# Down products by tokens in the second FFN, with the residual transposed into the banks and the last stage by tokens

## The chip, the cores and the metric

The kernel runs on one core of one Trainium2 chip. Its metric is the device time of one execution, in microseconds (us), given as the median of several runs. Engines are TensorE (PE; PEld is its weight load), VectorE (DVE), ScalarE (ACT), GpSimd (POOL) and SyncE (SP), which issues most DMAs.

## The reference, cut to what matters

Two transformer blocks on 256 tokens of width 1024. The change touches the end of the second: a gated FFN with a causal convolution (2816 hidden channels) and the per-layer gate behind it.

```python
    u = causal_dwconv(rmsnorm_2(x, g_ffn) @ w_up, ffn_conv_w)
    u_gate, u_val = jnp.split(u, 2, axis=-1)
    x = x + (jax.nn.silu(u_gate) * u_val) @ w_down

    x = x + jax.nn.sigmoid(rmsnorm_2(x, g_ple) @ w_ple_gate) * (p_i.astype(x.dtype) @ w_ple)
    return x
```

`rmsnorm_2(x, g)` is x times g over the root of the mean square of a token's 1024 channels. All is float32.

## The kernel before

**Arithmetic.** Each float32 operand of a large product is split in two parts, `hi` (fp32r) and `lo` (the rest). `product` (lines 1076 to 1081) makes three matmuls of one product: its first operand is stationary in TensorE, its second moves, hi by hi (L1079), hi by lo (L1080) and lo by hi (L1081).

**Layout.** The residual `XT` is held by channels: partition = channel within a tile of 128, free dimension = tile and 256 tokens. In `gemm` a weight tile of 128x128 is stationary and 256 tokens move. A chunk of weights is 2048 columns for each partition (1 MB). Chunks pass through three rings of three buffers: SP loads `raw`, ACT writes `whi` (`split_hi`, L572), DVE writes `wlo` (`split_lo`, L581). `adv(name)` splits the chunk that lies three places behind `name`; it waits until `name`'s products are done, by `multiplied`.

**Second FFN.** For each of 11 steps `j`: gate chunk `sg`, value chunk `sa` (48 matmuls each, in a ring of two banks, 0 and 1), then the down chunk `sd` of step j-2 (`down`: 2 tiles `t` of hidden channels by 8 output tiles `nb` by 3 matmuls, accumulated over all steps in banks 4 to 7, each bank holding two output tiles by 256 tokens). ACT and DVE run the convolution and the silu. Ahead of it stand the sum of squares `sum4` (`sum_squares`, L1113) and ten filler products `keep_clock` (L1118), during which the residual is normalised.

**Last stage, as PE issues it.** The products of `p` by `w_ple` (`ple`, four units a to d of 12 matmuls), with the sum of squares `sum5` between b and c; four filler products; the gate products `pg0` to `pg3` (48 matmuls each); 16 transposes of the sum (L1694). Beside it DVE adds the down banks to `XT` (`add_x`, L2426); ACT squares them (L772); ACT takes the root (L607) and DVE the reciprocal of 128x256 values (L1726); DVE scales (L1736), ACT writes the hi parts (`norm_hi`, L622), DVE the lo parts (L1746), and only then can the gate products start. At the end ACT takes the sigmoid of each gate unit (L909, 128x512), DVE multiplies (L2477) and adds (L2478), PE transposes to tokens, ACT (L1043) and DVE (L2481) copy out of the banks, and SP stores two halves of 512 KB (L518).

Each engine runs its instructions in program order; all waits are on semaphores.

Of the kernel before, what the change touches and what calls it, by code (L numbers as in the profile page):

```python
# [22 lines left out]
ALU = mybir.AluOpType  # L23
# [6 lines left out]
P = 128  # L30
# [71 lines left out]
def build(nc, i, out):  # L102
# [66 lines left out]
    for c in range(4):  # L169
        chunk(f"pg{c}", cols(i["w_ple_gate_2"][0], 256 * c), (KT, 256))  # L170
    N_SPLIT = sum(not c[0] for c in CHUNKS)
# [34 lines left out]
    g_units += [(f"s{n}{j}", "dve") for j in range(FFT // 2) for n in "ga"]  # L206
    g_units += [(f"ple{c}", "act") for c in "abcd"] + [(f"pg{c}", "act") for c in range(4)]
    l_units = [(f"sa{n}", "dve") for n in range(2)] + [(f"sb{n}", "dve") for n in range(4)]
# [11 lines left out]
    m_units += [(n, "act") for n in ("lq0", "lq1", "lk0", "lk1", "sfq0", "sfq1", "sfk0", "sfk1")]  # L220
    m_units += [("pT", "dve"), ("on2", "act"), ("on3", "act"), ("sum4", "act"), ("sum5", "act")]

    with ExitStack() as ctx:
# [124 lines left out]
        PF = slot(16, 1, 0, 512)  # L348
        PLE = slot(18, 2).rearrange("p (k t) -> p k t", t=T)
        SMY, SMA, RB, NCF = (slot(19, 1, 256 * n, 256) for n in range(4))  # L350
# [13 lines left out]
        OUTN = slot(4, 2).rearrange("p (a d) -> p a d", a=2)  # L364
        PG = slot(2, 2).rearrange("p (k t) -> p k t", t=T)
        SQ2 = slot(0, 2)
        nf2 = small[:, 72:80]
        gain2 = small[:, 64:72]
# [42 lines left out]
        def multiplied(g):  # L411

            name = [n for n, k in G.items() if k == g][0]
            if name[0:2] in ("fd", "sd") and name[2:].isdigit():
                return down_used, int(name[2:]) + 1 + (FFT // 2 if name[0] == "s" else 0)
            unit = [n for n, _ in g_units if n == name or n[:-1] == name and n[-1] in "abcd"][-1]
            return g_full, g_no(unit) + 1
# [17 lines left out]
        def m_done(u):  # L435
# [16 lines left out]
            sem(n) for n in ("x_init", "y_f32", "y_hi", "y_lo", "p_hi", "p_lo", "merged_f32", "osq2", "qd_exp"))  # L452
        out_act, out_dve, acc2_start, silu2 = (sem(n) for n in ("out_act", "out_dve", "acc2_start", "silu2"))
        u2_f32 = sem("u2_f32")
# [7 lines left out]
        def _(sp):  # L462
# [71 lines left out]
        def _(pool):  # L534
# [51 lines left out]
        def _(act):  # L586
# [439 lines left out]
            def ple(n):  # L1026
                u = f"ple{'abcd'[n]}"
                g_wait(u)
                act.activation(PLE[:, 2 * n:2 * n + 2, :], two(g_bank(u)), ACT.Copy).then_inc(g_empty["act"], 1)
            squares(lambda c: (x_new, 8 + c + 1), dst=SQ2)  # L1030
            ple(0)
            ple(1)
            norm_std("sum5", T, D)
            ple(2)
            ple(3)
            norm_hi(HT2, 18)
            adv("sd10")
            adv("ple")
            for c in range(4):
                copy_unit(f"pg{c}", PG[:, 2 * c:2 * c + 2, :], ACT.Sigmoid)  # L1040
            for n in range(2):
                act.wait_ge(l_full, len(l_units) + 2 * n + 1)
                act.activation(OUTN[:, n, 0:512], bank[4 + 2 * n][:, :], ACT.Copy).then_inc(out_act, 1)  # L1043


        @block.tensor
        def _(pe):
# [608 lines left out]
            sum_squares("sum4", 8, T, SQ2)  # L1656
            keep_clock(bank[4], 10)
            for j in range(FFT // 2):
                if j == 0:
                    gemm_first("sg0", T, 20)  # L1660
                else:
                    gemm(f"sg{j}", T)
                gemm(f"sa{j}", T)
                if j > 1:
                    down(j - 2, "s")
            down(FFT // 2 - 2, "s")
            down(FFT // 2 - 1, "s")

            def ple(units):

                wh, wl = w_parts("ple", 2)
                for u in units:
                    o = g_open("ple" + u)
                    for n in range(2):
                        nb = 2 * "abcd".index(u) + n
                        for k in range(2):
                            ws = [x[:, k, P * nb:P * (nb + 1)] for x in (wh, wl)]
                            ins = product(o[:, T * n:T * (n + 1)], ws, (phi[:, k, :], plo[:, k, :]), k == 0, k == 1)
                    ins.then_inc(g_full, 1)
            pe.wait_ge(p_hi, 1)  # L1680
            pe.wait_ge(p_lo, 1)
            ple("ab")
            sum_squares("sum5", 12, T, SQ2)
            ple("cd")
            keep_clock(bank[4], 4)
            gemm_first("pg0", T, 24)
            for c in range(1, 4):
                gemm(f"pg{c}", T)

            for t in range(2):  # L1690
                for c in range(2):
                    pe.wait_ge(x_new, 12 + 2 * (c + 1))
                    for k in range(4):
                        ins = pe.transpose(bank[4 + 2 * t + c][:, P * k:P * (k + 1)],  # L1694
                                           XT[:, 4 * c + k, P * t:P * (t + 1)], ident)
                    ins.then_inc(l_full, 1)


        @block.vector
        def _(dve):  # L1700
# [764 lines left out]
            adv(f"sd{FFT // 2 - 2}")  # L2465
            for c in range(4):
                dve.wait_ge(*((down_bank, 4 + c) if c < 3 else (down_used, FFT)))
                add_x(2 * c, bank[4 + c]).then_inc(x_new, 1)
            dve.wait_ge(x_new, 12)
            normalise(HT2, 24, T, XT[:, :, 0:T], lambda k, n: par("g_ple", k=k), None, "sum5")  # L2470
            adv("sd10")
            adv("ple")
            for c in range(4):
                s_ = slice(2 * c, 2 * c + 2)
                adv(f"pg{c}")
                dve.wait_ge(*g_done(f"pg{c}"))
                link(dve.tensor_tensor(PG[:, s_, :], PG[:, s_, :], PLE[:, s_, :], ALU.mult))  # L2477
                dve.tensor_tensor(XT[:, s_, 0:T], XT[:, s_, 0:T], PG[:, s_, :], ALU.add).then_inc(x_new, 1)  # L2478
            for n in range(2):
                dve.wait_ge(l_full, len(l_units) + 2 * n + 2)  # L2480
                dve.tensor_copy(OUTN[:, n, 512:1024], bank[5 + 2 * n][:, :]).then_inc(out_dve, 1)  # L2481

# [24 lines left out]
```

## Time and profile before

| | us |
|---|---|
| median of 3 runs | 1045.29 (1043.66 to 1047.16) |
| profiled execution, its own time | 1041.31 |
| its span, first to last instruction | 1039.5 |
| PE busy in the span | 982.0 (94%) |
| DVE busy | 763.5 (73%) |
| ACT busy | 504.5 (49%) |

The profiled execution is 3.98 us below the median of the runs, and 1.81 us of its own time lie outside its span. The mean granted TensorE clock is 0.99 of full speed. A matmul's row gives its latency; matmuls overlap, so what one costs is the distance between starts.

### The profile page before, as it was taken

How to read it: one execution, taken by the hardware profiler on the slowest of the kernel's cores; microseconds unless marked ns; L12 is line 12 of the kernel's file. 1: busy time of each engine (PE TensorE's matmuls, PEld its weight loads, DVE VectorE, ACT ScalarE, POOL GpSimd, SP SyncE). 2: the span in 40 equal slices, each digit the busy share in tenths (PEclk: the TensorE clock that was granted, in tenths of full speed). 3: DMA queues.
4: the chain of work that ended last, by engine and by line, in shares of the span. 5: the costliest groups of instructions: out<-in, count | busy, mean ns of one | idle time of the engine just before them, and what ended most of it. 6: DMA issues, size and time to landing. Idle time of an engine off the chain costs nothing.

```text
span 1039.5 us, 17879 instructions
## 1 busy us (share of the span) xinstructions
PE 982.0 (94%) x7608; PEld 937.9 (90%) x7608; DVE 763.5 (73%) x1106; ACT 504.5 (49%) x619; POOL 14.8 (1%) x31
## 2 busy tenths in 40 slices
PE   5899999998899999998998999999989999999997
PEld 3478999898899999998897889999989999999997
DVE  5679997877978898867959967544675776666664
ACT  5544434525554565447734553323544645454552
POOL 0000000002000000000100000000000000000000
PEclk9999999999999999999999999999999999999999
DMA  9787443345275567656766774635454455555521
GB/s 339 239 287 246 154 162 116 129 155 173 95 253 188 190 209 243 163 122 122 134 166 107 172 161 90 117 90 107 130 183 142 143 183 191 174 192 173 195 89 41
DMA packets 144094, 170.57 MB, mean 164 GB/s; under 512 B 3120, under 2 KB 133440, under 8 KB 144016
## 3 DMA queue, kind: packets, MB, share of 16 engines
q1 hardware_dynamic: 142112, 165.63, 54.5%
q10 hardware_dynamic: 1200, 2.43, 0.6%
q0 software_dynamic: 704, 1.39, 0.5%
q8 instruction: 60, 0.98, 0.4%
q14 instruction: 18, 0.15, 0.0%
HBM read 168.37 MB, written 1.05 MB: 163 GB/s over the span
## 4 chain that ended last, share of the span: by engine, by line
PE 58%; DVE 11%; ACT 4%; issue 3%; DMA 2%; DVEq 0%; ACTq 0%
PE bank L1079 17%; PE bank L1080 17%; PE bank L1081 17%; PE bank L1549 4%; DVE wlo L581 3%; ACT whi L572 2%; DMA raw<-in_w_in_dram 2%; DVE arena L2191 1%; DVE arena L2059 1%; DVE arena L1736 1%; DVE arena L2152 1%; PE bank L1113 1%; DVE arena L2221 1%; DVE arena L1726 1%; ACT arena L916 0%
## 5 line engine op out<-in xcount | busy, mean ns | idle before, releaser
L1079 PE MATMUL bank<-hhi,whi 128*128 128x256 f32 (+1 forms) x2000 | 581.7, 291 | 23.9 <-DVE arena L2152 4.8
L1080 PE MATMUL bank<-hlo,whi 128*128 128x256 f32 (+1 forms) x2000 | 574.8, 287 | 0.0
L1081 PE MATMUL bank<-hhi,wlo 128*128 128x256 f32 (+1 forms) x2000 | 574.6, 287 | 0.0
L1079 PEld LDWEIGHTS bank<-hhi,whi 128*128 128x128 f32 x2000 | 385.5, 193 | 33.7 <-issue 24.0
L581 DVE TENSOR_TENSOR wlo<-raw,whi 128x2048 fp32r<-128x2048 f32 x131 | 299.6, 2289 | 144.2 <-ACT whi L572 103.8
L1080 PEld LDWEIGHTS bank<-hlo,whi 128*128 128x128 f32 x2000 | 385.6, 193 | 3.8 <-issue 1.2
L1081 PEld LDWEIGHTS bank<-hhi,wlo 128*128 128x128 f32 x2000 | 385.5, 193 | 2.5
L572 ACT ACTIVATE whi<-raw 128x2048 fp32r<-128x2048 f32 x131 | 250.3, 1911 | 123.5 <-PE bank L1081 69.1
L2059 DVE SCALAR_TENSOR_TENSOR arena<-arena,params 128x256 f32<-128x256 f32 x176 | 71.5, 479 | 5.8 <-ACT arena L801 5.8
L2444 DVE SCALAR_TENSOR_TENSOR arena<-bank,params,arena 128x255 f32<-128x255 f32 (+1 forms) x88 | 36.4, 476 | 31.9 <-ACT arena L1012 31.6
L909 ACT ACTIVATE arena<-bank 128x512 f32<-128x512 f32 x22 | 13.2, 598 | 91.9 <-PE bank L1081 91.9
L1012 ACT ACTIVATE arena<-bank,params 128x256 f32<-128x256 f32 x44 | 18.5, 470 | 61.1 <-PE bank L1081 61.1
L1549 PE MATMUL bank<-arena 128*128 128x128 f32 x336 | 40.0, 275 | 1.4 <-DVE arena L2321 1.4
L1549 PEld LDWEIGHTS bank<-arena 128*128 128x128 f32 x336 | 38.8, 192 | 1.6 <-DVE arena L2321 1.6
L1079 PE MATMUL bank<-whi,hhi 128*128 128x256 f32 x128 | 37.1, 290 | 0.0
L1081 PE MATMUL bank<-whi,hlo 128*128 128x256 f32 x128 | 36.2, 283 | 0.0
L1080 PE MATMUL bank<-wlo,hhi 128*128 128x256 f32 x128 | 36.2, 283 | 0.0
L772 ACT ACTIVATE arena<-XT 128x512 f32<-128x512 f32 x16 | 10.0, 631 | 42.7 <-DVE XT L2023 23.2
L1827 DVE SCALAR_TENSOR_TENSOR raw<-raw,small 128x256 f32<-128x256 f32 x72 | 29.5, 480 | 0.0
L1079 PEld LDWEIGHTS bank<-whi,hhi 128*128 128x128 f32 x128 | 24.5, 192 | 0.2 <-issue 0.2
L1080 PEld LDWEIGHTS bank<-wlo,hhi 128*128 128x128 f32 x128 | 24.5, 192 | 0.2 <-issue 0.2
L1081 PEld LDWEIGHTS bank<-whi,hlo 128*128 128x128 f32 x128 | 24.5, 192 | 0.0
(326 smaller groups left out, 886.7 us busy)
## 6 DMA issues: line engine op xcount, KB each, us to landing
raw<-in_w_in_dram SPq DMA_DIRECT2D x46, 1024.0 KB, 8.4
raw<-in_w_up_dram SPq DMA_DIRECT2D x44, 1024.0 KB, 5.1
raw<-in_w_down_dram SPq DMA_DIRECT2D x22, 1024.0 KB, 4.9
raw<-in_w_ada_dram SPq DMA_DIRECT2D x19, 1024.0 KB, 5.3
raw<-in_w_branch_dram SPq DMA_DIRECT2D x6, 1024.0 KB, 5.1
arena<-in_w_ada_dram SPq DMA_DIRECT2D x10, 512.0 KB, 9.3
raw<-in_w_out_dram SPq DMA_DIRECT2D x4, 1024.0 KB, 5.1
raw<-in_w_o_dram SPq DMA_DIRECT2D x4, 1024.0 KB, 5.1
```

The lines of the kernel that those rows point to most:

```text
L572: act.activation(whi[:, g % RING, :], raw[:, n % RING, :], ACT.Copy).then_inc(w_hi, 1)
L581: dve.tensor_tensor(wlo[:, g % RING, :], raw[:, n % RING, :], whi[:, g % RING, :].bitcast(F32), ALU.subtract).then_inc(w_lo, 1)
L909: act.activation(dst, two(g_bank(u)), func).then_inc(g_empty["act"], 1)
L1012: ins = act.activation(acc2[:, b, n, t, :], g_bank(f"s{w}{j}")[:, T * t:T * (t + 1)], ACT.Copy, scale=col)
L1079: pe.matmul(o, wh, ah, start=start, stop=False, **kw)
L1080: pe.matmul(o, wh, al, start=False, stop=False, **kw)
L1081: return pe.matmul(o, wl, ah, start=False, stop=stop, **kw)
L1113: ins = pe.matmul(o[:, 0:w], ones, src[:, w * k:w * (k + 1)], start=k == 0, stop=k == KT - 1)
L1549: ins = pe.matmul(o[:, P * h:P * (h + 1)], lhsT(c, h), rhs(c, h), start=True, stop=True)
L1827: ins = dve.scalar_tensor_tensor(out=w[:, k % 2, :], in0=w[:, k, :], scalar=silu_c[:, k, 0:1], in1=w[:, k % 2, :], op0=ALU.mult, op1=ALU.add)
L2059: ins = dve.scalar_tensor_tensor(out=a, in0=pad[:, b, t, dy:dy + 4, dx:dx + 64], scalar=par("conv_w", k=FFT * tap + 2 * j + t), in1=a, op0 ...
L2444: ins = dve.scalar_tensor_tensor(out=acc2[:, b, n, t, d:T], in0=ps[:, T * t:T * (t + 1) - d], scalar=par("ffn_conv", k=2 * FFT * (2 - d) + ...
```

## The change

- `down_tokens` takes the place of `down` in the second FFN: a slice of 128 tokens of `u` is stationary, and 512 columns of the down weights move. A chunk is 2 tiles `t` by 2 token halves `a` by 2 column halves `c` by 3 = 24 matmuls. Banks 4 to 7 now hold 128 tokens by 512 channels.
- The residual is not added by DVE at the end: ahead of the FFN, behind `sum4`, 16 transposes put it into banks 4 to 7 (the first of each bank starts it), and the down products accumulate on top. Filler products there go from ten to six.
- The last stage is by tokens. DVE makes `XG` = bank times `g_ple` (a row spread over all partitions by a new DMA that POOL issues behind `sum4`). ACT sums squares of the banks with `accum_out`, takes a root of 2 columns, DVE a reciprocal of 2 columns. PE transposes `XG` (`tokens_turn`, four units of 4 transposes); ACT and DVE split the result. The reciprocal root is not multiplied in ahead of the gate products; it is the `scale` of the sigmoid. `sum5`, the four filler products, `normalise` and `norm_hi` of this stage go.
- `ple` and the gate products have tokens stationary and 512 columns moving (24 and 96 matmuls for all). The gate chunks are cut as 4 row tiles by 512 columns. Gate units are `gate{c}{t}`: column half c, token half t; both banks of a c are opened ahead of its first product.
- The sum with the bank is written by DVE straight to `OUTN`, with no transposes and no copies, and stored in four pieces of 256 KB.

```diff
-    m_units += [("pT", "dve"), ("on2", "act"), ("on3", "act"), ("sum4", "act"), ("sum5", "act")]
+    m_units += [("pT", "dve"), ("on2", "act"), ("on3", "act"), ("sum4", "act")] + [(f"hT{n}", "dve") for n in range(4)]
...
-            for t in range(2):
-                sp.wait_ge(out_act, t + 1)
-                sp.wait_ge(out_dve, t + 1)
-                sp.dma_start(o[:, t, :], OUTN[:, t, :]).then_inc(stored, 16)
-            sp.wait_ge(stored, 32)
+            for c in range(2):
+                for t in range(2):
+                    sp.wait_ge(out_dve, 2 * c + t + 1)
+                    s = slice(512 * c, 512 * (c + 1))
+                    sp.dma_start(o[:, t, s], OUTN[:, t, s]).then_inc(stored, 16)
+            sp.wait_ge(stored, 64)
...
+            pool.wait_ge(m_full, m_no("sum4") + 1)
+            r = ROWS["g_ple"]
+            pool.dma_start(ple_gain, i["table"][r:r + 8, :].rearrange("r f -> (r f)").partition_broadcast(P)
+                           ).then_inc(gain_loaded, 16)
...
+            square_sums(0)
+            adv("sd10")
             ple(0)
             ple(1)
-            norm_std("sum5", T, D)
+            tokens_hi(0)
             ple(2)
             ple(3)
-            norm_hi(HT2, 18)
-            adv("sd10")
+            tokens_hi(1)
             adv("ple")
-            for c in range(4):
-                copy_unit(f"pg{c}", PG[:, 2 * c:2 * c + 2, :], ACT.Sigmoid)
-            for n in range(2):
-                act.wait_ge(l_full, len(l_units) + 2 * n + 1)
-                act.activation(OUTN[:, n, 0:512], bank[4 + 2 * n][:, :], ACT.Copy).then_inc(out_act, 1)
+            square_sums(1)
+            act.wait_ge(std5_ready, 1)
+            act.activation(rstd5, rstd5, ACT.Sqrt, bias=eps, scale=1.0 / D).then_inc(std5_ready, 1)
+            adv("pg0")
+            act.wait_ge(rstd5_ready, 1)
+            for c in range(2):
+                for t in range(2):
+                    u = f"gate{c}{t}"
+                    g_wait(u)
+                    act.activation(PG[:, t, 512 * c:512 * (c + 1)], g_bank(u)[:, :], ACT.Sigmoid,
+                                   scale=rstd5[:, t:t + 1]).then_inc(g_empty["act"], 1)
...
-            keep_clock(bank[4], 10)
+            pe.wait_ge(*g_done("wp3"))
+            for t in range(2):
+                for c in range(2):
+                    for k in range(4):
+                        pe.matmul(bank[4 + 2 * t + c][:, P * k:P * (k + 1)], XT[:, 4 * c + k, P * t:P * (t + 1)],
+                                  ident, start=k == 0, stop=False, is_transpose=True, skip_group_check=True)
+            keep_clock(m_bank("hT0"), 6)
+
+            def down_tokens(j):
+
+                b = j % 3
+                wh, wl = w_parts(f"sd{j}", 2)
+                pe.wait_ge(u_hi, FFT // 2 + j + 1)
+                pe.wait_ge(u_lo, FFT // 2 + j + 1)
+                last = j == FFT // 2 - 1
+                order = [(t, a, c) for a in range(2) for c in range(2) for t in range(2)] if last else \
+                        [(t, a, c) for t in range(2) for a in range(2) for c in range(2)]
+                for t, a, c in order:
+                    tok = [u[:, b, t, P * a:P * (a + 1)] for u in (uhi, ulo)]
+                    ws = [x[:, t, 512 * c:512 * (c + 1)] for x in (wh, wl)]
+                    ins = product(bank[4 + 2 * a + c][:, :], tok, ws, False, last and t == 1, skip_group_check=True)
...
             ple("ab")
-            sum_squares("sum5", 12, T, SQ2)
+            tokens_turn(0)
             ple("cd")
-            keep_clock(bank[4], 4)
-            gemm_first("pg0", T, 24)
-            for c in range(1, 4):
-                gemm(f"pg{c}", T)
-
-            for t in range(2):
-                for c in range(2):
-                    pe.wait_ge(x_new, 12 + 2 * (c + 1))
-                    for k in range(4):
-                        ins = pe.transpose(bank[4 + 2 * t + c][:, P * k:P * (k + 1)],
-                                           XT[:, 4 * c + k, P * t:P * (t + 1)], ident)
-                    ins.then_inc(l_full, 1)
+            tokens_turn(1)
+
+            for c in range(2):
+                o = [g_open(f"gate{c}{t}")[:, :] for t in range(2)]
+                for part in range(2):
+                    wh, wl = w_parts(f"pg{2 * c + part}", 4)
+                    for t, k in [(t, k) for t in range(2) for k in range(4)]:
+                        kk = 4 * part + k
+                        if c == 0 and k == 0:
+                            pe.wait_ge(h_hi, 24 + 2 * t + part + 1)
+                            pe.wait_ge(h_lo, 24 + 2 * t + part + 1)
+                        ins = product(o[t], acts(T, kk, P * t, P), [x[:, k, :] for x in (wh, wl)], kk == 0,
+                                      kk == KT - 1, skip_group_check=True)
...
+            dve.wait_ge(gain_loaded, 16)
+            for n in range(4):
+                dve.wait_ge(*((down_bank, 4 + n) if n < 3 else (down_used, FFT)))
+                s_ = slice(512 * (n % 2), 512 * (n % 2) + 512)
+                dve.tensor_tensor(XG[:, n // 2, s_], bank[4 + n][:, :], ple_gain[:, s_], ALU.mult).then_inc(x_new, 1)
             adv("sd10")
...
+            tokens_lo(0)
+            tokens_lo(1)
             adv("ple")
...
+            dve.wait_ge(ss5_ready, 4)
+            dve.tensor_tensor(rstd5.unsqueeze(2), ss5.rearrange("p (a c) -> p a c", c=2)[:, :, 0:1],
+                              ss5.rearrange("p (a c) -> p a c", c=2)[:, :, 1:2], ALU.add).then_inc(std5_ready, 1)
+            dve.wait_ge(std5_ready, 2)
+            dve.reciprocal(rstd5, rstd5).then_inc(rstd5_ready, 1)
+            adv("pg0")
+            for c in range(2):
+                for t in range(2):
+                    s_ = slice(512 * c, 512 * (c + 1))
+                    dve.wait_ge(*g_done(f"gate{c}{t}"))
+                    link(dve.tensor_tensor(PG[:, t, s_], PG[:, t, s_], PLE[:, t, s_], ALU.mult))
+                    dve.tensor_tensor(OUTN[:, t, s_], PG[:, t, s_], bank[4 + 2 * t + c][:, :], ALU.add
+                                      ).then_inc(out_dve, 1)
```

## Rows read from the trace of the kernel before

**Rows 1.** The page, busy time and share of the span for each engine.

```profile
PE 982.0 (94%) x7608; PEld 937.9 (90%) x7608; DVE 763.5 (73%) x1106; ACT 504.5 (49%) x619; POOL 14.8 (1%) x31
```

**Rows 2.** Windows: stretch, length, busy PE PEld DVE ACT POOL, clock, DMA share, GB/s.

```profile
40.00:50.00 10.00, 8.08 (x34) 4.22 (x35) 4.01 (x3) 4.76 (x7) 0.00 (x0) 0.83 0.11 31
817.00:995.00 178.00, 178.00 (x1486) 178.00 (x1485) 119.63 (x138) 87.43 (x96) 0.00 (x0) 1.00 0.55 184
1000.00:1039.00 39.00, 32.32 (x251) 30.88 (x249) 21.11 (x26) 15.00 (x18) 0.00 (x0) 1.00 0.07 28
```

**Rows 3.** Groups of PE's matmuls by shape; the moving operand is named first.

```profile
L1079 PE MATMUL bank<-hhi,whi 128*128 128x256 f32 x1936 | 556.7, 288 | 22.7 <-DVE arena L2152 4.8 <-issue 4.6 <-ACT whi L572 3.7
L1079 PE MATMUL bank<-whi,hhi 128*128 128x256 f32 x128 | 37.1, 290 | 0.0
L1079 PE MATMUL bank<-hhi,whi 128*128 128x512 f32 x64 | 25.1, 391 | 1.3 <-DVE hlo L1751 0.7 <-ACT arena L674 0.6
```

**Rows 4.** Timeline of PE in the first projection, matmuls of 512 columns: start, length.

```profile
59.93 0.39 PE L1081 MATMUL bank<-hhi,wlo 128*128 128x512 f32 x1
...
63.33 0.39 PE L1081 MATMUL bank<-hhi,wlo 128*128 128x512 f32 x1
64.31 0.47 PE L1079 MATMUL bank<-hhi,whi 128*128 128x512 f32 x1 [0.59 <-ACT arena L674]
```

**Rows 5.** Timeline of PE ahead of the second FFN.

```profile
797.18 3.62 PE L1113 MATMUL bank<-arena,cf 128*128 128x256 f32 x16
800.63 4.48 PE L1118 MATMUL bank<-cf 128*128 128x256 f32 x20
805.62 0.36 PE L1079 MATMUL bank<-hhi,whi 128*128 128x256 f32 x1 [0.51 <-ACT hhi L622]
```

**Rows 6.** Timeline of PE in the last stage.

```profile
995.77 0.28 PE L1079 MATMUL bank<-hhi,whi 128*128 128x256 f32 x1
...
998.65 3.62 PE L1113 MATMUL bank<-arena,cf 128*128 128x256 f32 x16
...
1007.16 0.36 PE L1079 MATMUL bank<-hhi,whi 128*128 128x256 f32 x1 [0.29 <-DVE hlo L1746]
...
1012.87 0.28 PE L1081 MATMUL bank<-hhi,wlo 128*128 128x256 f32 x1
1014.16 0.36 PE L1079 MATMUL bank<-hhi,whi 128*128 128x256 f32 x1 [1.01 <-ACT whi L572]
...
1031.38 0.28 PE L1081 MATMUL bank<-hhi,wlo 128*128 128x256 f32 x1
...
1033.80 1.53 PE L1694 MATMUL bank<-cf,XT 128*128 128x128 f32 x12 [1.70 <-DVE XT L2478]
```

**Rows 7.** Timeline of ACT around and in the last stage.

```profile
990.27 1.92 ACT L572 ACTIVATE whi<-raw 128x2048 fp32r<-128x2048 f32 x1 [3.33 <-PE bank L1081]
...
999.46 1.28 ACT L607 ACT_TABLE_LOAD   x1
...
1031.70 0.60 ACT L909 ACTIVATE arena<-bank 128x512 f32<-128x512 f32 x1 [5.16 <-PE bank L1081]
```

**Rows 8.** Timeline of DVE around and in the last stage.

```profile
992.27 2.29 DVE L581 TENSOR_TENSOR wlo<-raw,whi 128x2048 fp32r<-128x2048 f32 x1 [2.87 <-ACT whi L572]
994.48 2.48 DVE L2426 TENSOR_TENSOR XT<-bank,XT 128x512 f32<-128x512 f32 x4
...
1033.05 0.69 DVE L2478 TENSOR_TENSOR XT<-XT,arena 128x512 f32<-128x512 f32 x1
...
1035.37 0.69 DVE L2481 COPY arena<-bank 128x512 f32<-128x512 f32 x1 [0.18 <-PE bank L1694]
```

**Rows 9.** A group of ACT's accumulator reads, in the first stage.

```profile
L639 ACT ACTIVATION_READ_ACCUMULATOR arena<-arena 128x1 f32 x4 | 0.8, 188 | 0.0
```

**Rows 10.** DMA issues by source: engine, count, size, median us to landing.

```profile
out_dram<-arena SPq DMA_DIRECT2D x2, 512.0 KB, 2.8
arena<-in_w_spatial_dram SPq DMA_DIRECT2D x1, 256.0 KB, 4.9
```

More of the change, by code:

```diff
@@ L169, in build @@
     for c in range(4):
-        chunk(f"pg{c}", cols(i["w_ple_gate_2"][0], 256 * c), (KT, 256))
+        chunk(f"pg{c}", rows(i["w_ple_gate_2"][0], 4 * (c % 2), 4)[:, :, 512 * (c // 2):512 * (c // 2 + 1)], (4, 512))
     N_SPLIT = sum(not c[0] for c in CHUNKS)
@@ L206, in build @@
     g_units += [(f"s{n}{j}", "dve") for j in range(FFT // 2) for n in "ga"]
-    g_units += [(f"ple{c}", "act") for c in "abcd"] + [(f"pg{c}", "act") for c in range(4)]
+    g_units += [(f"ple{c}", "act") for c in "abcd"] + [(f"gate{c}{t}", "act") for c in range(2) for t in range(2)]
     l_units = [(f"sa{n}", "dve") for n in range(2)] + [(f"sb{n}", "dve") for n in range(4)]
@@ L1664, in _ @@
                 if j > 1:
-                    down(j - 2, "s")
-            down(FFT // 2 - 2, "s")
-            down(FFT // 2 - 1, "s")
+                    down_tokens(j - 2)
+            down_tokens(FFT // 2 - 2)
+            down_tokens(FFT // 2 - 1)
             def ple(units):
@@ L1673, in ple, with tokens_turn @@
                     o = g_open("ple" + u)
[L1674 to L1678, printed above, removed]
-                    ins.then_inc(g_full, 1)
+                    c, t = divmod("abcd".index(u), 2)
+                    s = slice(512 * c, 512 * (c + 1))
+                    for k in range(2):
+                        ws = [x[:, k, s] for x in (wh, wl)]
+                        tok = [x[:, k, P * t:P * (t + 1)] for x in (phi, plo)]
+                        ins = product(o[:, :], tok, ws, k == 0, k == 1)
+                    ins.then_inc(g_full, 1)
+            def tokens_turn(a):
+                for half in range(2):
+                    n = 2 * a + half
+                    o = m_bank(f"hT{n}")
+                    if n >= 2:
+                        pe.wait_ge(h_lo, 24 + n - 1)
+                    pe.wait_ge(x_new, 8 + n + 1)
+                    for k in range(4):
+                        ins = pe.transpose(o[:, P * k:P * (k + 1)], XG[:, a, 512 * half + P * k:512 * half + P * (k + 1)],
+                                           ident)
+                    ins.then_inc(m_full, 1)
             pe.wait_ge(p_hi, 1)
@@ L2465, in _ @@
             adv(f"sd{FFT // 2 - 2}")
[L2466 to L2470, printed above, removed]
-            adv("sd10")
-            adv("ple")
[L2473 to L2478, printed above, removed]
@@ new lines, in _, with tokens_lo @@
+            adv("sd10")
+            def tokens_lo(a):
+                for half in range(2):
+                    n = 2 * a + half
+                    dve.wait_ge(h_hi, 24 + n + 1)
+                    s_ = slice(4 * half, 4 * half + 4)
+                    dve.tensor_tensor(h_tok[1][:, s_, a, :], four(m_bank(f"hT{n}")),
+                                      h_tok[0][:, s_, a, :].bitcast(F32), ALU.subtract).then_inc(h_lo, 1)
+            tokens_lo(0)
+            tokens_lo(1)
+            adv("ple")
@@ new lines, in _ @@
+            dve.wait_ge(ss5_ready, 4)
[4 more added lines that the diff above has]
+            adv("pg0")
+            for c in range(2):
+                for t in range(2):
[4 more added lines that the diff above has]
+                                      ).then_inc(out_dve, 1)
```

39 lines of the change are left out of this document (31 added, 8 removed).

## The prediction

> **What bounds the kernel now.** I read the page's busy times first, then windows over the second FFN and the last stage, then PE's groups by shape, then the timelines of PE, ACT and DVE at the seams. PE is busy 94% of the span [rows 1]. Over the second FFN the window of 178 us shows PE busy for all 178, at a clock of 1.00, with DVE busy for 120 and ACT for 87 [rows 2]: there only PE's own work can shorten the time, and the others have about a third of theirs free. From 1000 us to the end it is otherwise: PE is busy for 32.3 of 39 us [rows 2], and the time goes into a chain through four engines. So the two places need two kinds of sum: spacing of matmuls in the one, a chain in the other.
>
> **What a matmul costs.** Its row's length (288 ns at 256 columns, 391 at 512 [rows 3]) is latency. The spacing counts: in the window 1486 matmuls start in 178.00 us, 0.120 us each [rows 2]. At 512 columns there are 15 starts between 59.93 and 63.33 us: 3.40 / 15 = 0.227 us [rows 4]. So two of 256 cost 0.240 and one of 512 costs 0.227, 0.013 less. That the weights now move does not matter by itself: the group with weights moving and tokens stationary has 290 ns against 288 [rows 3].
>
> The difference of 0.013 is what the FFN part hangs on, and a rule bears on it. The Trainium skill (TensorE: Matmul & The Clock Gate, Back-to-back issue gap) gives an isolated gap of columns / 2.4 GHz plus 2.5 ns, by which merging two matmuls saves only 2.5 ns. The rows show 13, so I go by them; by the page the sum below would be smaller by 384 pairs x 0.0108 = 4.1 us, an estimate from that page.
>
> **1. Down products.** A down chunk goes from 48 x 0.120 = 5.76 to 24 x 0.227 = 5.44 us; 11 chunks save 3.5 us. PE has no idle time there [rows 2], so all of it shows, if nothing new makes PE wait. A freed buffer is split by ACT in 1.92 and DVE in 2.29 us [rows 7, 8], 4.3 us with the hand-overs, and the chunk is wanted two chunks later (11.2 us now, 11.5 before): about 7 us of cover. The FFN's `u` is still wanted two steps later. Bounds: 0 (512 columns cost 0.240) to 3.5.
>
> **2. Ahead of the second FFN.** Transposes: 12 take 1.53 us with the latency of the last and one restart [rows 6], so 0.11 to 0.13 each, and 16 cost 1.8 to 2.0 us. Removed: 4 of 10 filler products, 4.48 us for ten [rows 5], so 1.8 us. Both lie ahead of a wait for the normalised residual that already ends last (PE idles 0.51 us, then starts at 805.62 [rows 5]): 0, bounds 0.3 either way. The gain's DMA is issued by POOL, which has nothing behind it, some 190 us before DVE wants it; a 256 KB load took 4.9 us [rows 10], so 512 KB is hidden. Uncovered it would be some 5 to 10 us.
>
> **3. Until the gate products start.** Before, from the first `ple` matmul (995.77, call it 0) to the first gate matmul (1007.16) it is 11.39 us [rows 6]: `ple` a and b 2.88, `sum5` 3.3, c and d 3.0, fillers and wait 2.2.
>
> After, by engines, same zero. DVE is late first: the lo part of `pg0` waits for ACT's, which waits for `sd9`'s products (over at -5.3): ACT to -3.3, DVE to -0.9 (before, the same pair ran from 990.27 to 994.56 [rows 7, 8]). The four `XG` products read a bank like L2426, which took 2.48 us for four [rows 8]: -0.9 to 1.5. ACT's two squares wait for the first two, each 0.63 plus an accumulator read of 0.19 [rows 9]: done at 1.4. Then the hi part of `pg1`, 1.92: 3.3. Behind it `ple` a and b are copied, 0.60 each, the length of L909 [rows 7]: 3.9 and 4.5; then the two hi copies of half 0, to 5.6. DVE makes `pg1`'s lo part to 5.7 and the lo parts of half 0 to 6.3 and 6.9. PE: `ple` a and b, 12 x 0.227 = 2.7; eight transposes to 3.7; unit c needs a's bank copied out: starts at 4.05, a stall of 0.4; c and d to 6.8; the transposes of half 1 need banks freed by DVE at 6.3 and 6.9, so they run to 7.7. First gate product at 7.8. Its second token half needs DVE again at 10.5 and has it at 9.5. Saved: 11.4 - 7.8 = 3.6 us. Bounds: 4.4, when the stall and the waits vanish (PE's own work is 5.4 + 1.8 = 7.2 us), to 2.0, when each of four hand-overs is late by 0.4.
>
> **4. The gate products.** Before, from 1007.16 to the last one's start at 1031.38 it is 24.22 us [rows 6]: 191 spacings of 0.120 = 22.9 and one stall for `pg1`'s split (1012.87 to 1014.16, 1.2 us too long [rows 6]). That stall goes, since `pg1` is split at 5.7 and wanted at 13.2. After: 95 x 0.227 = 21.6. But a new wait comes: both banks are opened before c=1, and the second is still being filled until c=0 ends. So PE waits out latency 0.39 [rows 4], a sigmoid of 0.60 [rows 7] and two hand-overs of about 0.15, less one spacing: 0.9 us; the first projection has such a wait at the same shape, 63.33 to 64.31, 0.75 too long [rows 4]. Queued behind it is all of c=1; nothing else waits. 21.6 + 0.9 + 0.1 (first matmul slow) = 22.6: 1.6 saved, bounds 0.3 (no gain by columns) to 1.8. Covered beside it: ACT's hi parts of `pg2` and `pg3`, two squares, the root and two table loads of 1.28 [rows 7], between 7.6 and 17.1, while the first gate unit is full at 16.2. So its sigmoid is about 1 us late, but the bank that PE waits for is the second, full at 19: cover 1.4 us, beyond which each late us costs one.
>
> **5. Behind the last product.** Before: from 1031.38 to DVE's last copy (1035.37 + 0.69) 4.68 us, through sigmoid, multiply, add, 12 transposes, copy [rows 6 to 8]. After: latency 0.39, sigmoid 0.60, multiply 0.69, add from the bank 0.69, three hand-overs of 0.03: 2.5. Saved 2.2 (1.9 to 2.3). The store: before, 1039.5 - 1036.06 = 3.4 us; its DMA took 2.8 to land with 512 KB, now 256 KB [rows 10]: 0.2 saved, 0 to 0.6.
>
> **Sum.** 3.5 + 0 + 3.6 + 1.6 + 2.2 + 0.2 = 11.1 us. The span goes from 1039.5 to 1028.4. The profiled execution (1041.31) stood 3.98 us below the median of the runs; I take that distance as kept: 1045.29 - 11.1 = 1034.2 us.
>
> **The rivals.**
>
> *Columns give nothing.* In the FFN, unlike in the first projection, DMA, ACT and DVE work on the rings all the time, and moving 512 columns of a ring buffer may cost 0.240. Against it: the first projection splits chunks too, and holds 0.227 [rows 4]. It gives 3.5 + 1.3 + 0.3 less: 6.0 saved, 1039.3. The page's 2.5 ns would end near there (1038.3, an estimate from the Trainium skill's TensorE: Matmul & The Clock Gate). Chance 0.12.
>
> *ACT and DVE pace the last stage.* ACT has squares, two hi parts of chunks, eight copies, roots and sigmoids in one program order, and PE's transposes wait for DVE behind it. If each hand-over in part 3 is late by its bound and the first sigmoids by 1 us beyond their cover, 2.6 us are lost: 1036.8. For it: the chain leaves DVE and PE within 0.1 us of each other at 6.9. Against: before, ACT is busy only 15 of 39 us there [rows 2]. Chance 0.14.
>
> *The clock falls (the other side).* Where PE idled and ran small work, at 40 to 50 us, the granted clock was 0.83 [rows 2]: 1.7 us' worth lost, at the lower level of 1.2 GHz half of 3.4 us. Transposes take the place of full products at two places here. One such fall costs 1.7 us, both 3.4: 1037.6. To turn the change into a loss it has to hold: at 1.2 GHz a matmul of 512 columns takes 0.427 instead of 0.227, so 14.2 us (11.1 and the 3.1 that can be told) need 71 of the last stage's 120 below. All 120 low would cost 24 us: 1058. Against it: the clock was 1.00 from 1000 to 1039 us with 16 transposes and two waits for them [rows 2, 6]. The Trainium skill (TensorE: Matmul & The Clock Gate, PE-mode transpose) says that transposes don't raise the clock as products do; no row contradicts it, and it is why this case is not at zero. One short fall 0.03, held low 0.03.
>
> **How the numbers follow.** Forecast (1032.5 to 1036.0) 0.61, columns 0.12, ACT and DVE 0.14, clock 0.06, something that no row shows 0.07. All bounds at their worst save 3.9 us (1041.4), all at their best 12.9 (1032.4); the runs of before scatter by 1.7 either way, which takes the lower end to 1030.7, and the worst of all at once is unlikely, so the range is 1030.7 to 1040.0. A measurement of this kernel can tell about 0.3%, 3.1 us. Faster by more: all but the low clock, a part of the unknown and the tail of the two mild rivals, 0.89; within it 0.07; slower 0.04.
>
> **What would show it.** Down groups of 512 columns spaced by 0.227 with no idle from 817 to some 991 us (part 1). First gate product 7.8 us behind the first `ple` matmul, with short waits for ACT's copy and for DVE's lo part (3). One wait of some 0.9 us for a sigmoid halfway through 96 gate matmuls and none for a split (4). From the last matmul's start to DVE's last add 2.5 us (5). A clock of 1.00 at both seams. It is wrong if the spacing is 0.24, if PE idles for over 1 us before the gate products, or if a window of the last stage shows a clock well under 1.

## The result and the profile after

The changed kernel takes 1028.38 us in the median of 4 runs (1026.38 to 1029.27); before, 1044.47 us beside it (4 runs). The ratio is 0.9842, 95% interval [0.9819, 0.9866]. The forecast was 1034.2, range 1030.7 to 1040.0: the way is right, and the time lies 2.3 us below the range. The profiled execution has its own time of 1029.27 and a span of 1027.5 us, 12.0 less than before's.

So two numbers want an account: the profiled spans differ by 12.0 us, where the sum gave 11.1, and the medians by 16.1.

PE's groups by shape in the changed kernel, from 800 us on, answer to [rows 3]:

```profile
L1114 PE MATMUL bank<-hhi,whi 128*128 128x256 f32 x352 | 99.6, 283 | 0.5 <-ACT hhi L635 0.5
L1114 PE MATMUL bank<-whi,hhi 128*128 128x512 f32 x128 | 50.2, 392 | 0.8 <-ACT arena L1077 0.8
```

The 128 per line are 88 of the down products, 8 of `ple` and 32 of the gates. One line has all of PE's new idle time: 0.8 us for a sigmoid. The window over the FFN answers to [rows 2]:

```profile
812.00:990.00 178.00, 178.00 (x1259) 167.91 (x1258) 122.08 (x143) 89.80 (x99) 0.00 (x0) 1.00 0.57 188
```

PE has no idle time and a clock of 1.00, as before, with 1259 matmuls in 178 us (1486 in a window of that length before). The windows over the two seams, up to PE's last matmul, have a clock of 1.00 as well:

```profile
800.00:812.00 12.00, 11.52 (x85) 10.74 (x85) 9.24 (x14) 5.19 (x8) 0.55 (x1) 1.00 0.27 94
990.00:1023.00 33.00, 32.07 (x148) 26.01 (x146) 17.69 (x20) 17.07 (x26) 0.00 (x0) 1.00 0.17 55
```

The timeline of PE at both seams answers to [rows 5, 6] (start, length):

```profile
797.23 3.62 PE L1148 MATMUL bank<-arena,cf 128*128 128x256 f32 x16
800.68 1.91 PE L1696 MATMUL bank<-cf,XT 128*128 128x128 f32 x16
802.43 2.76 PE L1153 MATMUL bank<-cf 128*128 128x256 f32 x12
805.67 0.36 PE L1114 MATMUL bank<-hhi,whi 128*128 128x256 f32 x1 [0.48 <-ACT hhi L635]
...
992.50 0.39 PE L1114 MATMUL bank<-whi,hhi 128*128 128x512 f32 x1
...
995.22 1.03 PE L1749 MATMUL bank<-cf,arena 128*128 128x128 f32 x8
996.01 0.48 PE L1114 MATMUL bank<-whi,hhi 128*128 128x512 f32 x1
...
999.75 0.47 PE L1114 MATMUL bank<-whi,hhi 128*128 128x512 f32 x1
...
1011.73 0.47 PE L1114 MATMUL bank<-whi,hhi 128*128 128x512 f32 x1 [0.82 <-ACT arena L1077]
...
1022.51 0.39 PE L1116 MATMUL bank<-whi,hlo 128*128 128x512 f32 x1
```

Ahead of the FFN nothing moved: 16 transposes (1.8 us) stand where four filler products stood, and the same wait ends at 8.44 us behind the first square product in both kernels. The first `ple` matmul starts at 992.50, the first gate matmul at 999.75, and c=1 waits once, at 1011.73. The ends of ACT and DVE answer to [rows 7, 8]:

```profile
1022.93 0.69 ACT L1077 ACTIVATE arena<-bank,small 128x512 f32<-128x512 f32 x1 [2.03 <-PE bank L1116]
```

```profile
1024.38 0.69 DVE L2572 TENSOR_TENSOR arena<-arena,bank 128x512 f32<-128x512 f32 x1
```

And the stores, answering to [rows 10]:

```profile
out_dram<-arena SPq DMA_DIRECT2D x4, 256.0 KB, 2.0
```

The stages, each read as a difference of two starts in the two profiles:

| stage | before | after | saved | forecast |
|---|---|---|---|---|
| FFN, first product to first `ple` | 190.15 | 186.83 | 3.3 | 3.5 |
| to the first gate product | 11.39 | 7.25 | 4.1 | 3.6 |
| to the start of the last gate product | 24.22 | 22.76 | 1.5 | 1.6 |
| to DVE's end | 4.68 | 2.56 | 2.1 | 2.2 |
| to the end of the span | 3.4 | 2.4 | 1.0 | 0.2 |
| all, from the FFN's first product on | 233.9 | 221.8 | 12.1 | 11.1 |

I call the last line the tail and what lies ahead of it the head. The head is 805.6 and 805.7 us in the two profiles, and no kernel below changes its code. The 4 us by which the medians differ more than the tails must lie there, or in a tail that the profiled executions don't show.

### The profile page after: what moved, and what is told of

It reads as the page before. It is cut to its first block, busy times and chain, and to the rows that moved or that the text cites. A ratio compares the mean times of both kernels' runs of the same rounds, so it can differ in the third digit from the quotient of the medians.

```text
span 1027.5 us, 17077 instructions
## 1 busy us (share of the span) xinstructions
PE 978.5 (95%) x7208; PEld 919.9 (90%) x7208; DVE 757.4 (74%) x1097; ACT 502.9 (49%) x621; POOL 15.3 (1%) x32
## 4 chain that ended last, share of the span: by engine, by line
PE 59%; DVE 10%; ACT 4%; issue 3%; DMA 1%; DVEq 0%; ACTq 0%
PE bank L1114 18%; PE bank L1115 17%; PE bank L1116 17%; PE bank L1584 4%; DVE wlo L594 3%; ACT whi L585 1%; DVE arena L2268 1%; DMA raw<-in_w_in_dram 1%; DVE arena L2136 1%; DVE arena L2229 1%; DVE arena L2298 1%; DVE arena L1813 1%; PE bank L1459 0%; ACT arena L929 0%; PE bank L1153 0%
## 5 line engine op out<-in xcount | busy, mean ns | idle before, releaser
L1114 PE MATMUL bank<-hhi,whi 128*128 128x256 f32 (+1 forms) x1744 | 510.1, 292 | 20.4 <-DVE arena L2229 4.4
L1115 PE MATMUL bank<-hlo,whi 128*128 128x256 f32 (+1 forms) x1744 | 503.8, 289 | 0.0
L1116 PE MATMUL bank<-hhi,wlo 128*128 128x256 f32 (+1 forms) x1744 | 503.5, 289 | 0.0
L1114 PEld LDWEIGHTS bank<-hhi,whi 128*128 128x128 f32 x1744 | 337.6, 194 | 29.7 <-issue 21.2
L1115 PEld LDWEIGHTS bank<-hlo,whi 128*128 128x128 f32 x1744 | 337.8, 194 | 4.0 <-issue 1.2
L1116 PEld LDWEIGHTS bank<-hhi,wlo 128*128 128x128 f32 x1744 | 337.8, 194 | 2.5
L1114 PE MATMUL bank<-whi,hhi 128*128 128x256 f32 (+1 forms) x256 | 87.3, 341 | 0.8 <-ACT arena L1077 0.8
L1115 PE MATMUL bank<-wlo,hhi 128*128 128x256 f32 (+1 forms) x256 | 86.1, 336 | 0.0
L1116 PE MATMUL bank<-whi,hlo 128*128 128x256 f32 (+1 forms) x256 | 86.1, 336 | 0.0
L1114 PEld LDWEIGHTS bank<-whi,hhi 128*128 128x128 f32 x256 | 48.6, 190 | 6.3 <-ACT arena L1077 1.2
```

The costliest lines, as they stand in the source:

```text
L1114: pe.matmul(o, wh, ah, start=start, stop=False, **kw)
L1115: pe.matmul(o, wh, al, start=False, stop=False, **kw)
L1116: return pe.matmul(o, wl, ah, start=False, stop=stop, **kw)
```

## The experiments

**The same two kernels again, many times** (`before_again`, `after_again`, no edit).

> The kernel before, unchanged, against itself. What is open: the profiled executions differ by 12.0 us (1039.5 to 1027.5), the medians by 16.1. Theory A, chance: the profiled execution of before was one of its quicker ones, and the executions of both scatter in stages ahead of 800 us; then this median is 1041 to 1045, and a second profile has the same lengths as the first behind 805 us (190.2 us of FFN, 43.7 to the end) and differs ahead of it. Theory B, the kernel before loses some us in its last stage or FFN in most executions, by a lower clock at its idle seams, and the first profile did not show it: the median is near 1044.5 and the second profile is longer behind 805 us by 2 to 5 us. Ratio to itself 1.000 in both.

> The changed kernel, unchanged, on the same chip. Theory A: its median stands 12 us below that of before (ratio 0.9885), within some 2 us. Theory B: 16 us below (ratio 0.985), and its own spans scatter less than those of before.

Measured: `before_again` 1043.21 us (12 runs), ratio to before 0.9995 [0.9979, 1.001]; `after_again` 1028.19 (5 runs), 0.9841 [0.9819, 0.9864]. The 16 us are real. The profiled tails repeat to 0.03 us: 233.9 and 221.8. Each run also lists its span. Span less tail gives the head, if an execution without a profile has the tail of the profiled ones, which nothing here can check directly: for before 808.5 us in the median of 43 executions (805.4 to 813.8), for the changed kernel 804.6 in 9 (801.8 to 807.2). So the first profile of before, with a head of 805.6, was a quick execution, and the changed kernel's, with 805.7, a slow one. Theory B has no support in these profiles: both tails of each kernel are alike, in clock and in idle time. Theory A explains the scatter, but not that the median of the head falls by 3.9 us in code that is the same.

**Columns alone** (`cols256`): each new product as two of 256 columns.

```diff
+            def product_halves(o, w, a, start, stop, **kw):
+                kw = dict(kw, skip_group_check=True)
+                for s in (slice(0, 256), slice(256, 512)):
+                    ins = product(o[:, s], w, [x[:, s] for x in a], start and s.start == 0, stop, **kw)
+                return ins
...
-                    ins = product(bank[4 + 2 * a + c][:, :], tok, ws, False, last and t == 1, skip_group_check=True)
+                    ins = product_halves(bank[4 + 2 * a + c], tok, ws, False, last and t == 1, skip_group_check=True)
```

(and the same for `ple` and the gates)

> All of the change, but each product of 512 moving columns is made as two of 256 (down products, ple and gate products; 384 pairs). My account: 0.240 instead of 0.227 us for each pair, so 5.1 us longer than the changed kernel: FFN 190.1 instead of 186.8 us, gates 1.3 longer. Rival (the page's isolated gap, 2.5 ns for each matmul): about 1 us longer in all. If the doubled weight loads become the bound, over 8 us longer.

Measured: tail 226.55 us, 4.7 longer; time 1038.29 (6 runs). The window over the FFN (PE's count as before):

```profile
815.00:993.00 178.00, 178.00 (x1486) 178.00 (x1485) 121.92 (x142) 88.16 (x98) 0.00 (x0) 1.00 0.56 184
```

From its first product at 809.68 to the first `ple` matmul it takes 190.15 us, as before: the FFN's whole gain is columns, 0.013 us a pair, and the layout by tokens by itself gains nothing there. The isolated gap that the prediction cited from the Trainium skill (TensorE: Matmul & The Clock Gate, Back-to-back issue gap) would have made 1.0, an estimate (384 times 2.5 ns); the rows decide for 4.7. The time is 10.1 above the changed kernel's, again more than the tail: the head is back at 809.9 (6 executions).

**The new wait** (`open_late`): each gate bank is opened where its first product stands.

```diff
-                o = [g_open(f"gate{c}{t}")[:, :] for t in range(2)]
+                o = [None, None]
...
+                        if part == 0 and k == 0:
+                            o[t] = g_open(f"gate{c}{t}")[:, :]
```

> The changed kernel, but the bank of a gate unit is opened where its own first product stands, so the second bank of c=1 is wanted 12 matmuls (2.7 us) later, when its sigmoid is long done. My account of the new wait: the whole 0.8 us idle ahead of L1114 for ACT's sigmoid goes, 0.9 us less than the changed kernel. Rival: the first bank's sigmoid is late too (it waits for the table and pg3's split) and a wait of 0.3 to 0.8 us stays.

Measured: tail 220.61, 1.2 shorter, and PE's rows behind the transposes have no wait left. The whole wait went, so its reading was right and its price (0.9) a little low: the gate products alone take 21.6 instead of 22.8 us from the first start to the last. The median, 1028.96 (5 runs, head 806.5), can't tell it from the changed kernel.

**The deferred root** (`wait_root`): PE waits for the reciprocal root ahead of the gate products.

```diff
             tokens_turn(1)
+            pe.wait_ge(rstd5_ready, 1)
```

> The changed kernel, but PE waits for the reciprocal root ahead of the gate products, as the kernel before did, instead of taking it as the scale of the sigmoid. In the changed kernel that root is ready 5.7 us behind the first gate product. My account: part behind the FFN's first product 221.8 + 5.7 + about 0.1 = 227.6 us, less up to 1.5 us where the later sigmoids no longer wait (rival: PE's clock falls in the 5.7 us, then 1 to 3 us more).

Measured (one run): tail 229.2, 7.4 longer. PE's timeline, and a window behind the wait:

```profile
1005.33 0.79 PE L1114 MATMUL bank<-whi,hhi 128*128 128x512 f32 x1 [5.57 <-DVE small L2566]
```

```profile
1005.00:1007.00 2.00, 1.67 (x4) 1.38 (x5) 0.17 (x1) 0.08 (x1) 0.00 (x0) 0.50 0.00 0
```

5.57 us are the wait; the rival holds for the rest. After PE had stood idle the granted clock was 0.50, the level of 1.2 GHz, and the first matmuls start 0.43 us apart instead of 0.23. The gate products take 24.4 us from the first start to the last instead of 22.8, which is most of the other 1.8. Taking the root as the sigmoid's scale is worth this much in this order of work.

**The store** (`store2`): two stores of 512 KB.

```diff
-            for c in range(2):
-                for t in range(2):
-                    sp.wait_ge(out_dve, 2 * c + t + 1)
-                    s = slice(512 * c, 512 * (c + 1))
-                    sp.dma_start(o[:, t, s], OUTN[:, t, s]).then_inc(stored, 16)
-            sp.wait_ge(stored, 64)
+            for t in range(2):
+                sp.wait_ge(out_dve, 2 + t + 1)
+                sp.dma_start(o[:, t, :], OUTN[:, t, :]).then_inc(stored, 16)
+            sp.wait_ge(stored, 32)
```

> The changed kernel with two stores of 512 KB, as before, in place of four of 256 KB. I had given the smaller last store 0.2 us and the profile showed 1.0 (3.4 to 2.4 us from DVE's end to the end of the span). If it is the size that counts, 1.0 us comes back: 222.8 us behind the FFN's first product. If it is that the two last stores of before lay close together and shared the queues (0.9 us apart; here 2.7 us), 222.8 too but with the distance: so the first store's own time tells, 2.8 us before; if it stays at 2.8 with the larger distance, size counts.

Measured (one run): tail 222.4, 0.6 longer.

```profile
out_dram<-arena SPq DMA_DIRECT2D x2, 512.0 KB, 2.6
```

The last store decides. Before, the two stores were issued 0.9 us apart and landed after 2.6 and 3.0 us (median 2.8 in [rows 10]); here, 2.7 us apart, both take 2.6; at 256 KB the last takes 2.0. So of the 1.0 us, 0.6 is size and 0.4 goes with the distance between the stores. No run changed the distance at one size alone, in one kernel.

**The clock at the first seam** (`after_nofill`): `keep_clock(m_bank("hT0"), 6)` is left out.

> The changed kernel without its six filler products ahead of the second FFN. PE then idles some 3.2 us there (802.4 to 805.7) behind transposes. If transposes and the rest hold the clock, nothing moves: 221.8 us from the FFN's first product. The rival of the prediction (the clock falls there): a window of 805 to 812 us well under 1.00 and up to 1.7 us more behind the first product.

Measured (one run): PE idles 3.07 us behind the transposes, the window from 805 to 812 us has a clock of 1.00, the tail is 221.85. So the clock did not fall at this seam even without the fillers, in this one run; in `wait_root`, behind 5.6 us of idle time, it did.

**Where the other 4 us come from.** ACT's program ahead of 805 us is the same in all kernels, so its n-th instruction marks one place. Cut at such places, the profiles agree from program to program to about 1 us but for low-clock stretches, except in one part, the projections and scores of the second block's attention, 490 to 578 us (L861 to L916 of ACT in before). There ACT waits for loads of `w_in_2`. Waits of ACT from 526 to 564 us, before (waited for: total, times, longest):

```profile
ACT whi L572 <- DMA raw<-in_w_in_dram: 8.9, 2, 6.6
```

and in the changed kernel:

```profile
ACT whi L585 <- DMA raw<-in_w_in_dram: 4.5, 2, 3.7
```

ACT waits half as long for them, and the part takes 87.1 to 87.6 instead of 90.7 and 90.8 us. Not every load is sooner: counted from the start of the part, the load issued at 10.2 us lands at 24.4 instead of 21.6, while the one that ACT waits for longest lands at 53.7 instead of 56.9 and the next at 56.4 instead of 59.6 (before and the first profile of the changed kernel). What can the end of a program do to loads 250 us earlier? What the slower `cols256` shares with before, and not with the changed kernel, is the number of matmuls.

`after_pad` puts 200 products of one column behind the last gate product; `after_pad48` and `after_pad200` put 24 and 100 there. Each is two records. They run behind the part, so only their being in the program can act on it.

```diff
+            for _ in range(200):
+                pe.matmul(bank[2][:, 0:1], ones, ones[:, 0:1], start=True, stop=True)
```

> The changed kernel with 200 products of one column behind the last gate product (400 records, as many as the change took off PE), which write a bank that nobody reads. They add some 26 us from the last product on, of which some 5 lie beside the epilogue. The question is the stretch ahead of the second FFN, whose code no kernel here changes: measured span less the profiled length from the FFN's first product to the end. It was 808.5 us in the median for before, 810 for cols256 (as many matmuls as before), 804.7 for the changed kernel and 806 for open_late. Theory C (the amount of PE code sets how the loads of the fox stage fall, and with it this stretch): 808 to 811 here. Theory D (this stretch differs by chance from program to program, or by something else in the change): about 805, or no pattern.

> The changed kernel with 24 products of one column behind the last gate product, 48 PE records more: 7256, as in before_cut. Theory C: 42 to 43.5 us in the fox stretch. Theory D: 38 to 40.

> As after_pad48, with 100 such products, 200 PE records more: 7408. Theory C with a step between 7208 and 7256: 43 us in the fox stretch. If 7256 gives 38 and 7408 gives 43, the step lies elsewhere. Theory D: 38 to 40.

`before_cut` is the kernel before with the second FFN's down products as hi by hi (their lo products are left out); `before_cut2` also cuts `ple` so, and eight fillers.

```diff
+                    if tag == "s":
+                        ins = pe.matmul(o, ws[0], uhi[:, b, t, :], start=first and nb % 2 == 0, stop=last and t == 1,
+                                        skip_group_check=True)
+                    else:
```

> The kernel before with the down products of the second FFN reduced to hi by hi (16 instead of 48 matmuls for each chunk, 352 fewer in all; the two others are left out). FFN 42 us shorter: the part behind the FFN's first product goes from 233.9 to some 192 us. Theory C: the stretch ahead of it falls from 808 to 804 to 806 us, as in the changed kernel, though nothing of the change is in it. Theory D: it stays at 808.

> The kernel before with 400 PE records fewer, as many as the change takes off: the second FFN's down products and the ple products as hi by hi only, and eight filler products fewer there (the lo products are left out). What is looked at is the stretch of the fox stage from 526 to 564 us (two fixed places of ACT's program), which no kernel here changes: 43.6 and 43.6 us in the two profiles of before, 43.1 in cols256, 43.4 in after_pad (7608 records each), 42.6 in before_cut (7256), but 38.1 to 40.1 in the five profiles with 7208. Theory C, the amount of PE's code decides: 38 to 40 us here. Theory D, something else of the change decides (the new DMA of POOL, the other order on ACT and DVE): 43 us.

`after_poolpad` adds code on POOL instead, `after_short` has the changed kernel's new products as hi by hi, and two kernels add a tensor in device memory that takes part in nothing (512 bytes are written to it).

```diff
+            for _ in range(800):
+                pool.wait_ge(wsm_zero, 1)
```

> The changed kernel with 800 waits that are already satisfied at the end of POOL's program, which has nothing else to do from there on: about as much code as the 400 PE records (each a matmul and a weight load). If the whole amount of code decides, the fox stretch goes from 38 to 43 us; if PE's own does, it stays at 38 to 40. Behind the FFN's first product 221.8 us, unless POOL's waits last longer than the kernel.

> The changed kernel with its down, ple and gate products as hi by hi only (the lo products are left out): 256 PE records fewer, 6952. The stretch of the fox stage from 490 to 578 us (two fixed places of ACT's program) was 90.5 to 90.8 us with 7608 records, 88.0 with 7408, 87.7 and 88.2 with 7256, 86.7 to 87.6 with 7208. If it goes on falling with PE's code: 84 to 86.5. If it has an end at 7208: 87.

```diff
+    args["spare"] = nc.dram_tensor("aa_spare_dram", (1, 12800), _mybir.dt.float32, kind="Internal").ap()
```

> The changed kernel with an unused tensor of 51 KB in device memory, declared ahead of the inputs (a DMA of 512 B writes to it behind sum4). 51 KB is what the change takes off PE's code. If the code's length acts by where the weights come to lie behind it, the fox stretch (490 to 578 us) may go from 87.3 towards 90.6 us. If it stays at 87.3, that is not shown to be the way.

> As after_dram50k with 4 MB. Placement: the stretch changes by over 1 us either way. Otherwise 86.7 to 87.6 us.

Measured in each profile, from ACT's one fixed place to the other:

| PE matmul records | kernels | that part, us | DMA share, 490 to 578 us |
|---|---|---|---|
| 7608 | before, twice | 90.8, 90.7 | 0.67, 0.68 |
| 7608 | after_pad | 90.6 | 0.68 |
| 7592 | cols256 | 90.5 | 0.68 |
| 7408 | after_pad200 | 88.0 | 0.77 |
| 7256 | before_cut, after_pad48 | 88.2, 87.7 | 0.83, 0.84 |
| 7208 | before_cut2 | 86.7 | 0.88 |
| 7208 | changed kernel twice, open_late, wait_root, store2, after_poolpad | 87.6, 87.1, 87.2, 87.3, 87.0, 87.2 | 0.86, 0.87, 0.86, 0.87, 0.86, 0.87 |
| 7208 | after_dram50k, after_dram4m | 87.6, 87.1 | 0.85, 0.87 |
| 7196 | after_nofill | 87.4 | 0.86 |
| 6952 | after_short | 86.3 | 0.90 |

The expectations of `before_cut2`, `after_pad48`, `after_pad200` and `after_poolpad` go by a shorter stretch, which begins 34 to 36 us into this part and lasted 43.6 us in before. There they measured 39.5, 40.5, 40.6 and 40.0: no step up to 43 at 7256 or 7408, where I had expected one. That stretch also moves with the clock (`after_dram50k` has 42.0 in it), so I compare by the longer part. The longer part is not free of the clock either, but in five profiles the clock is 1.00 from 490 to 578 us, and they keep the order: `after_pad` 90.6, `after_pad48` 87.7, `open_late` and `after_poolpad` 87.2, `before_cut2` 86.7. Nor is it the chip: of the profiles taken on one chip, `cols256` has 90.5 and `after_again` 87.1, and on another `after_pad` has 90.6 and `before_cut` 88.2.

The changed kernel, padded to before's number, shows before's waits for the loads; this is the same view and stretch as the two above:

```profile
ACT whi L585 <- DMA raw<-in_w_in_dram: 8.7, 2, 6.4
```

So Theory C holds, and D falls: the part follows the amount of PE's code, with the change's code (`after_pad`) and without (`before_cut2`). My first reading of it as a step was wrong: the DMA share rises with every cut of the program, though 2.5 of the 3.3 us between 7592 and 7208 records lie above 7408. 800 more waits in POOL's program did not count (87.2), nor did a tensor more in memory, in one profile each. Windows from 490 to 578 us show what differs, before and `before_cut2`:

```profile
490.00:578.00 88.00, 79.18 (x584) 72.61 (x584) 73.47 (x75) 45.35 (x53) 6.73 (x11) 0.98 0.67 138
```

```profile
490.00:578.00 88.00, 81.58 (x618) 75.89 (x617) 77.37 (x89) 48.81 (x64) 6.75 (x11) 1.00 0.88 147
```

With the shorter program the DMA engines are busy for 0.88 instead of 0.67 of the time and move 147 instead of 138 GB/s; PE starts 618 instead of 584 matmuls. The queues over the same window, before and `before_cut2` (packets, MB, share of 16 engines):

```profile
q1 hardware_dynamic: 11935, 12.04, 66.8%
q8 instruction: 5, 0.08, 0.3%
```

```profile
q1 hardware_dynamic: 12740, 12.85, 87.7%
```

A packet of the loads takes 79 ns in the mean before and 97 with the shorter program (16 engines times 88 us times the share, by the packets). So the single packets are slower, more of them are under way at a time, and the whole comes out faster. The packets that fetch instructions in this window are 5 in both, so it is not more fetching here. Why the length of PE's program does this is open, and so is whether its length counts or where the rest comes to lie behind it.

The medians of all heads differ by as much, with more scatter: 808.7 us in the median of 55 executions of kernels with 7592 or 7608 records, 805.2 in 21 with 7208 or 7196, 3.5 apart. Single kernels stray from it by 2 us (`after_pad` 806.9 in 6, where before, run beside it, has 809.7; its padding takes 80 us and the tail is known from one profile; `before_cut` 806.4 in 5; `open_late` 806.5 in 5), since the heads also hold short stretches at the lower clock that fall differently in each execution. So the heads alone would not settle Theory C; the part in the profiles does. The times: `after_pad` 1108.9 us, `before_cut` 1007.65; one run each of `after_pad48` 1030.98, `after_pad200` 1065.35, `before_cut2` 1002.13, `after_poolpad` 1028.76, `after_short` 987.34, `after_dram50k` 1032.55, `after_dram4m` 1028.79, `wait_root` 1036.52, `store2` 1029.25, `after_nofill` 1030.02. I had given 200 one-column products 26 us; they took 80, 400 records about 0.2 us apart, with a clock of 0.50 from 1040 to 1100 us. And `before_cut` has a tail of 198.6 us where I had expected 192.

## Why the prediction was right or wrong

**Part 1, columns: right.** 3.3 us against 3.5, with PE never idle; `cols256` gives it back exactly. The smaller isolated gap of the Trainium skill (TensorE: Matmul & The Clock Gate, Back-to-back issue gap) was rightly set aside. ACT is free for half of that window (87 busy of 178 us) and not for a third, which changes no term.

**Part 2, ahead of the FFN: right.** 8.44 us in both kernels. The clock held, with fillers and (one run) without.

**Part 3, until the gates: mechanism right, 0.5 us too careful.** The stall that I foresaw at unit c (0.4 us) is not there. ACT's two squares overlap, with their accumulator reads, to 1.3 us from the first's start to the last's end, where I had put 0.82 each in a row, so the bank was free in time. The rest of the chain came in the order written and about 0.5 us earlier, and PE was held by its own work only.

**Part 4, the gates: right.** 1.5 against 1.6, one wait halfway for a sigmoid, none for a split. `open_late` took the wait away and gained 1.2.

**Part 5: the epilogue right (2.1 against 2.2), the store mis-sized.** I gave the smaller store 0.2 with a bound of 0.6; it gained 1.0. Size gives 0.6 of it; the bound lacked the second effect: before, the last store took 3.0 us close behind another of 512 KB, and 2.6 with more distance.

**The sum, and the step that failed.** The tail fell by 12.1 against 11.1 us, each term inside its bounds but the store's. What put the time outside the range is the sentence on the median: "I take that distance as kept". It was not. With 12.1 us off the median of before beside it (1044.47) the time would be 1032.4, inside the range; the measured one is 4.0 less. The profiled execution of before lay 3.98 us below its median, that of the changed kernel 0.9 above. Two things are in it. One is scatter: heads differ by over 5 us from execution to execution of one kernel, and I carried one execution's luck over to another kernel's median as if it belonged to the kernel. It alone would not move a median. The other does: about 3.5 us of the head, in code that the change does not touch, which the prediction put at nothing without a reason. In the profiles this is the part from 490 to 578 us, 90.8 to 87.3 us; the medians of the heads give 3.9. 12.1 and 3.5 to 3.9 make the 16. That the shorter program of PE brings it is shown; by what way, is open.

**The rivals.** Columns give nothing: no, 4.7 us by `cols256`. ACT and DVE pace the last stage: no, PE never waited for them before the gates. The clock: it stayed at 1.00 in both seams; in this last stage it fell when `wait_root` made PE idle 5.6 us.

## What to carry to other kernels

Sum a change stage by stage between fixed instructions of two profiles: the stages here repeat to 0.03 us, while whole executions scatter by 5. A distance between one profiled execution and a median is luck and not a property to carry over; either leave it out or widen the range by the scatter of the runs. And when the measured gain exceeds what the touched stages show, mark the untouched ones by the n-th instruction of an engine and compare them too.

Where a normalising factor is one number per row of a product's output, taking it into the next activation's scale removes the whole chain of root and reciprocal from PE's path, here 5.6 us and a fall of the clock. Opening both banks of a pair ahead of the first product costs a wait that opening each at its own first product avoids.

## What the runs showed of the hardware

- A stretch that waits for loads got quicker when PE's program was shorter elsewhere: 90.6 us with 7608 matmul records (`after_pad`), 88.0 with 7408, 87.7 with 7256, about 87.2 with 7208, 86.3 with 6952; 800 more waits on POOL changed nothing. The DMA share there rose from 0.68 to 0.90, and a packet of the loads took 97 ns (`before_cut2`) instead of 79 (before).
- 16 transposes and 3.07 us of idle time left the granted clock at 1.00; behind 5.57 us of idle time it was 0.50 for the first 2 us (one run each).
- The last store of 256 KB landed in 2.0 us, of 512 KB in 2.6, and of 512 KB with another 0.9 us ahead of it in 3.0.
